# A three-term float32 output projection over 1024 frames: one stage at the end, seven half-size products per column pair instead of eight

## The chip, the cores and the metric

One core of a Trainium2 chip runs the whole layer in one launch. The metric is the device time of that launch in microseconds (us); lower is better.

## The reference, cut to what matters

The layer is a hybrid block: 1024 frames of 2048 features, 16 learned meta frames put ahead of them, one input projection, a causal pooling mixer and a sliding-window attention side by side, gates, and one output projection that is added to the input.

```python
h = concatenate([meta, x])                       # (16 + 1024, 2048)
hn = rmsnorm(h, norm_g)
pv, pg, q, k, v, ag = split(hn @ w_in)           # 1024, 1024, 1024, 128, 128, 1024 columns
pool_out = per group of 256 channels: (trailing mean over 2, 4, 8 or 16 frames - frame) @ pool_w, * pool_scale
attn_out = attention over chunks of 64 frames (own chunk, the one before, the meta frames), q and k
           normalised per head, softmax with a sink logit; 16 query heads, 2 key heads
mixed = concatenate([silu(pg) * pool_out, silu(ag) * attn_out])    # (1024, 2048)
return (h + mixed @ w_out)[16:]                  # w_out is (2048, 2048)
```

All data is float32. The products must keep nearly float32 accuracy, so both kernels split every operand into a high and a low part of the matmul type fp32r and sum three products: high by high, high by low, low by high.

## The kernel before, in words

**Tiling.** The frames are taken in two halves of 512 (the first with the 16 meta frames, 528 columns). Weights come in blocks of 128 rows x 512 columns (256 KB) through four slots: SyncE loads a block into `raw` (`load_block`, L337), ScalarE copies it to `wh` as the high part (`split_high`, L482 through `copy`), VectorE subtracts to get the low part `wl` (`split_low`, L820 through `sub`), and TensorE uses it for 12 matmuls of 512 columns. The splits run three blocks ahead of TensorE (`LEAD`); a load waits until the block four before it is split.

**Order of a half.** The order is written out by hand, engine by engine, in steps of one weight block:

1. *First tiles* (8 blocks, L1231 to L1236): key and value columns. In the first half the frames are transposed on TensorE as they arrive (`first_group`, L1209, four 128x128 transposes per slice k of 128 features), multiplied by the gain on ScalarE (L526) and split on VectorE (L856); this runs four slices ahead. The RMS factor is not applied to the frames: ScalarE sums the squares of each row (`stats`, L495), VectorE inverts (L874), and the factor is spread over the columns (`r_columns`, `r_transposes`, `r_rows`) and multiplied in after the projection.
2. *Query tiles* (32 blocks, L1176 to L1181), with the norms of keys and queries between them.
3. *Four groups* of 24 blocks: gates, pooling inputs, and between the blocks the attention of the group's heads; at the end of each group 12 matmuls of the pooling mixer (L1401 to L1403). GpSimd makes the trailing sums (L443 to L454).
4. *Output projection* (`project`, L1427 to L1429): four column blocks of 512, each over 16 row blocks of `w_out`, for 4 tiles of 128 frames: 4 x 16 x 4 x 3 = 768 matmuls of 128x512. `mixed` is split by `mix_high` and `mix_low`; the residual is added by `add_residual` (L1128) and GpSimd stores the result (L470).

**The second half's frames.** During the first half's output projection they are loaded (L394), normalised in place with their RMS factor and the gain (`stats`, `norm`, L834), transposed (`x_group`, L1192, 16 times four transposes) and split into the same memory as the first half's (`half2_h`, `half2_l`). So the second half needs no factor after the projection.

```python
half2_h = flat_h[:, 0:KT * HALF].rearrange("p (k c) -> p k c", c=HALF)      # rows of 512 columns
act_h = sb("act_h", [P, KT, COLS], f32r)                                    # rows of 528 columns
```

In the first half a matmul reads 512 of the 528 columns of a row, from column 16 on; tiles with the meta frames are two matmuls of 264.

Of the kernel before, what the change touches and what calls it, by code (L numbers as in the profile page):

```python
# [15 lines left out]
P = 128  # L17
D = 2048
KT = D // P
META = 16  # L20
SEQ = 1024
# [3 lines left out]
SUB = COLS // 2  # L25
# [16 lines left out]
YB_FREE = 4  # L42
# [10 lines left out]
OB = D // BLK  # L53
OUT_BLKS = OB * KT
NBLK = IN_BLKS + OUT_BLKS
ROWT = HALF // P
XG = 4

X_LOAD, RES_LOAD = 6, 10
X_AT = (10, 9)  # L60

K_ORDER = [0, 1, 2, 3, 4, 5, 8, 9, 10, 11, 12, 13, 6, 7, 14, 15]
UNITS = 4


FIRST_SPLITS = {0: (0,), 3: (1, 2), 7: (3, 4), 11: (5, 6), 15: (7,)}
FIRST_LOADS = ((0, 2), (2, 4), (4, 8), (8, 12), (12, 16))
# [8 lines left out]
V_N = V_G + KT  # L76


def hymba_layer(nc, xcat, norm_g, w_in, w_out, pool_w, vecs, consts, out):
# [6 lines left out]
    with ctx:  # L86
# [5 lines left out]


        act_h = sb("act_h", [P, KT, COLS], f32r)
        act_l = sb("act_l", [P, KT, COLS], f32r)
# [4 lines left out]
        kT = sb("kT", [P, CHUNK + HALF])  # L100
        vT = sb("vT", [P, CHUNK + HALF])
        k_meta = sb("k_meta", [P, META])
        v_meta = sb("v_meta", [P, META])
        pv_last = sb("pv_last", [P, PAIRS, META])
# [5 lines left out]
        xrs = sb("xrs", [P, 5])  # L110

        band_h = sb("band_h", [P, KVH, (NCH + 1) * BAND], f32r)
        band_x = sb("band_x", [P, KVH, (NCH + 1) * BAND], f32r)
        v_s = sb("v_s", [P, NCH, 2, HD], f32r)
        mix_x = sb("mix_x", [P, 2, BLK], f32r)


        vm = sb("vm", [96, 2, HD], f32r)
        pm = sb("pm", [96, QUAD * P], f32r)
        qs = sb("qs", [P, QUAD, 2, CHUNK], f32r)
        o_part = sb("o_part", [HD, BLK])
        pt = sb("pt", [P, QUAD, 2, P], f32r)
        d_h = sb("d_h", [P, 2, HALF], f32r)
        d_l = sb("d_l", [P, 2, HALF], f32r)
        pw_h = sb("pw_h", [P, BLK], f32r)
        pw_l = sb("pw_l", [P, BLK], f32r)

        pnm = sb("pnm", [P, QUAD, P // QUAD])
        smax = sb("smax", [P, QUAD])
        nmax = sb("nmax", [P, QUAD])
        den = sb("den", [P, QUAD])
        esink = sb("esink", [P, QUAD])
        dtot = sb("dtot", [P, QUAD])
        rden = sb("rden", [P, QUAD])
        hscale = sb("hscale", [P, PAIRS])
        row_buf = sb("row_buf", [P, 2 * COLS])


        scr = sb("scr", [P, 7168])

        x_t = [scr[:, 0:D], scr[:, D:2 * D]]

        x_first = [mixed[:, 4 * r:4 * r + 4, :].rearrange("p k c -> p (k c)") for r in range(ROWT)]
        x_meta = x_t[1][0:META, :]
        meta_sq = x_t[0][0:META, :]
        meta_g = scr[:, 0:KT * META].rearrange("p (k c) -> p k c", c=META)
        g_row = scr[:, 2 * D:3 * D]  # L150
# [4 lines left out]
        res2 = sb("res2", [P, 2, BLK])  # L155
        y = [scr[:, 3 * D:3 * D + BLK], scr[:, 3 * D + BLK:3 * D + 2 * BLK], res2[:, 0, :], res2[:, 1, :]]

        flat_h = act_h[:, :, :].rearrange("p k c -> p (k c)")
        flat_l = act_l[:, :, :].rearrange("p k c -> p (k c)")
        half2_h = flat_h[:, 0:KT * HALF].rearrange("p (k c) -> p k c", c=HALF)  # L160
        half2_l = flat_l[:, KT * COLS - KT * HALF:].rearrange("p (k c) -> p k c", c=HALF)

        def act_cols(h, k, c):

            if h == 0:
                return act_h[:, k, c], act_l[:, k, c]
            own = slice(c.start - META, c.stop - META)
            return half2_h[:, k, own], half2_l[:, k, own]

        mix_h = [band_h[:, 0, 64:64 + BLK], band_h[:, 1, 48:48 + BLK],  # L170
                 v_s[:, 0:4, :, :].rearrange("p c a d -> p (c a d)"),
                 v_s[:, 4:8, :, :].rearrange("p c a d -> p (c a d)")]
        mix_l = [band_x[:, 0, 160:160 + BLK], band_x[:, 1, 144:144 + BLK], mix_x[:, 0, :], mix_x[:, 1, :]]
# [26 lines left out]


# [5 lines left out]
        KB, VB = ((R[0], R[1]), (R[1],)), ((R[2], O), (R[2],))  # L207
# [4 lines left out]
        YB = [R[0][:, :], S[:, 0, :], S[:, 1, :], O]  # L212
        FB = [S[:, 0, :], S[:, 1, :], PT[:, :], PM[:, :]]
        XB = [R[1][:, :], R[2][:, :], PT[:, :], PM]

        ident = cst[:, C_ID:C_ID + P]

# [4 lines left out]
        s_g = sem("s_g")  # L222
# [3 lines left out]
        s_x = [sem(f"s_x{i}") for i in range(2)]  # L226
        s_raw = [sem(f"s_raw{i}") for i in range(RAW)]
        s_pw = sem("s_pw")
        s_res = [sem(f"s_res{i}") for i in range(ROWT)]
        s_out = [sem(f"s_out{i}") for i in range(ROWT)]  # L230
        s_last = sem("s_last")
        s_free = sem("s_free")
# [12 lines left out]
        s_xn = sem("s_xn")  # L245
# [59 lines left out]
        s_me = sem("s_me")  # L305
        s_mh = sem("s_mh")
        s_ml = sem("s_ml")
        s_y = sem("s_y")
        s_ye = sem("s_ye")
# [3 lines left out]
                    s_ex, s_pl, s_pve, s_pvr, *s_gv, *s_gt, s_free]  # L313

        block = ctx.enter_context(nc.Block())

        def product_done(eng, h, n):

            eng.wait_ge(s_blk, ONE + h * NBLK + n + TILE_BLKS)

# [11 lines left out]
        def _(sp):  # L332
# [14 lines left out]

            sp.dma_start(cst[:, 0:P], consts[:, 0:P]).then_inc(s_id, 16)
# [13 lines left out]
            for h in range(HALVES):  # L362
                h0 = h * NBLK
                for n in range(RAW if h == 0 else 0, KV_BLKS):
                    load_block(h0 + n, n % RAW, w_in[TILE_BLKS * (n % 2) + n // 2, :, :])
                with sp.Fori(0, PAIRS) as j:
# [4 lines left out]
                sp.wait_ge(s_free, ONE + h * OB * ROWT)  # L371
                with sp.Fori(0, GROUPS) as g:

# [6 lines left out]

                def out_loads(nb, frames):

                    for k in range(KT):
                        kk = K_ORDER[k]
                        load_block(h0 + IN_BLKS + nb * KT + k, k % RAW,
                                   w_out[kk * P:(kk + 1) * P, bass.ds(nb * BLK, BLK)])
                        if k == X_LOAD and frames is not None:

                            sp.wait_ge(s_me, ONE + (h + 1) * 2 * GROUPS)
                            sp.wait_ge(s_xt, 1 + XG * (ROWT - 1 + nb))  # L390
                        if X_LOAD <= k < X_LOAD + OB and frames is not None:

                            cols = slice((k - X_LOAD) * BLK, (k - X_LOAD + 1) * BLK)
                            sp.dma_start(x_t[frames][:, cols],  # L394
                                         xcat[bass.ds(HALF + META + P * nb, P), cols]).then_inc(s_x[frames], 16)
                        if k == RES_LOAD:

                            sp.wait_ge(s_me, ONE + (h + 1) * 2 * GROUPS)

                            sp.wait_ge(s_free, ONE + (h * OB + nb) * ROWT)  # L400
# [5 lines left out]
                if h == 0:  # L406
                    with sp.Fori(0, 2) as i:
                        for v in range(2):
                            nb = i * 2 + v
                            out_loads(nb, v)  # L410
# [1098 lines left out]
```

## Time and profile before

| | before |
|---|---|
| median of 3 runs | 1246.59 us (1245.5 to 1247.13) |
| profiled execution, its own time | 1246.73 us |
| its span, first to last instruction | 1244.9 us |
| TensorE busy | 1232.2 us, 99% |
| VectorE / ScalarE busy | 63% / 51% |
| DMA, mean | 108 GB/s |
| first half: first tiles, queries, groups, output projection end at | 42, 139, 461, 643 us |
| second half: first tiles, queries, groups, output projection end at | 665, 757, 1067, 1241 us |

In the windows of rows 3, the first is a stretch of the second half's groups, the second the last output stage, the third what is left after TensorE's last matmul. In the timeline a matmul's duration contains its pipeline; its price in a stream is the distance from its start to the next start. "Idle before" is an engine's gap ahead of an instruction, with what ended it.

### The profile page before, as it was taken

What the parts mean: (1) busy time and instruction counts of PE and PEld (TensorE: products, weight loads), DVE (VectorE), ACT (ScalarE), POOL (GpSimd) and SP (SyncE); (2) the same over time, 40 slices, a digit from 0 to 9 for tenths busy, and PEclk for the clock granted to TensorE, in tenths of its full rate; (3) what the DMA queues carried; (4) which work ended last, traced back from release to release, by engine and by line L of the source; (5) the groups of instructions that cost most, each with busy time, mean ns of one, the idle gap of its engine ahead of it and who ended that gap; (6) DMA issues with size and microseconds to landing.
All of it is one profiled execution on the core that took longest, in us unless ns stands there. A gap on an engine that the chain in (4) does not pass through costs nothing.

```text
span 1244.9 us, 19321 instructions
## 1 busy us (share of the span) xinstructions
PE 1232.2 (99%) x6210; PEld 1043.4 (84%) x6210; DVE 788.4 (63%) x1381; ACT 638.2 (51%) x1495; POOL 81.5 (7%) x94
## 2 busy tenths in 40 slices
PE   8999999999999999999999999999999999999998
PEld 7887798898988978888888888888888888888887
DVE  4677767576675775665644676675757657654553
ACT  4744465464564655545533444655646556444442
POOL 0000001020120210000000000000101103000000
PEclk9999999999999999999999999999999999999999
DMA  7223323322232225544533333332322322343442
GB/s 239 77 85 102 92 78 86 83 85 78 76 94 78 74 71 207 192 133 150 193 127 85 99 95 94 78 92 76 102 77 85 91 79 88 117 133 127 168 144 85
DMA packets 72817, 134.38 MB, mean 108 GB/s; under 512 B 8096, under 2 KB 11424, under 8 KB 72608
## 3 DMA queue, kind: packets, MB, share of 16 engines
q1 hardware_dynamic: 70368, 125.17, 33.0%
q0 software_dynamic: 2384, 8.39, 1.9%
q8 instruction: 35, 0.57, 0.2%
q14 instruction: 30, 0.25, 0.1%
HBM read 125.14 MB, written 8.39 MB: 107 GB/s over the span
## 4 chain that ended last, share of the span: by engine, by line
PE 93%; DVE 3%; ACT 2%; DMA 1%; issue 1%; SPq 0%; DVEq 0%; ACTq 0%
PE R L1176 16%; PE R L1177 16%; PE R L1181 16%; PE S L1427 5%; PE S L1429 5%; PE S L1428 5%; PE R L1429 2%; PE R L1427 2%; PE OP L1427 2%; PE OP L1429 2%; PE R L1428 2%; PE OP L1428 2%; PE OP L1352 1%; PE S L1327 1%; PE OP L1177 1%; PE OP L1176 1%
## 5 line engine op out<-in xcount | busy, mean ns | idle before, releaser
L482 ACT ACTIVATE wh<-raw 128x512 fp32r<-128x512 f32 x400 | 249.9, 630 | 428.6 <-PE R L1181 197.9
L820 DVE TENSOR_TENSOR wl<-raw,wh 128x512 fp32r<-128x512 f32 x400 | 279.7, 701 | 289.3 <-ACT wh L482 288.9
L1176 PE MATMUL R<-act_h,wh 128*128 128x512 f32 (+1 forms) x1056 | 385.3, 370 | 1.2 <-DVE wl L820 1.1
L1177 PE MATMUL R<-act_l,wh 128*128 128x512 f32 (+1 forms) x1056 | 381.5, 366 | 0.0
L1181 PE MATMUL R<-act_h,wl 128*128 128x512 f32 (+1 forms) x1056 | 365.1, 365 | 0.0
L1176 PEld LDWEIGHTS R<-act_h,wh 128*128 128x128 f32 x1056 | 198.7, 188 | 33.2 <-DVE wl L820 2.0
L1177 PEld LDWEIGHTS R<-act_l,wh 128*128 128x128 f32 x1056 | 198.7, 188 | 30.3
L1181 PEld LDWEIGHTS R<-act_h,wl 128*128 128x128 f32 x1056 | 190.2, 188 | 33.1
L454 POOL TENSOR_TENSOR scr<-scr 128x527 f32<-128x527 f32 (+3 forms) x40 | 50.2, 1254 | 379.2 <-ACT scr L482 325.5
L482 ACT ACTIVATE pm<-OP 16x128 fp32r<-16x128 f32 x256 | 68.3, 267 | 5.5
L820 DVE TENSOR_TENSOR pt<-PT,pt 128x512 fp32r<-128x512 f32 x32 | 22.1, 692 | 59.9 <-ACT pm L482 59.9
L943 DVE RECIPROCAL scr<-scr 128x512 f32<-128x512 f32 x16 | 53.5, 3346 | 3.2 <-ACT scr L634 2.4
L820 DVE TENSOR_TENSOR qs<-mixed,qs 64x256 fp32r<-64x256 f32 x64 | 26.9, 421 | 39.6 <-ACT qs L482 39.1
L1427 PE MATMUL S<-wh,band_h 128*128 128x512 f32 x128 | 49.9, 390 | 0.0
L1427 PE MATMUL S<-wh,v_s 128*128 128x512 f32 x128 | 49.9, 390 | 0.0
L1429 PE MATMUL S<-wh,band_x 128*128 128x512 f32 x128 | 49.9, 390 | 0.0
L1429 PE MATMUL S<-wh,mix_x 128*128 128x512 f32 x128 | 49.9, 390 | 0.0
L1428 PE MATMUL S<-wl,v_s 128*128 128x512 f32 x128 | 49.8, 389 | 0.0
L1428 PE MATMUL S<-wl,band_h 128*128 128x512 f32 x128 | 49.8, 389 | 0.0
L701 ACT ACTIVATE scr<-S,nmax 128x144 f32<-128x144 f32 x128 | 47.0, 379 | 0.7
L820 DVE TENSOR_TENSOR mix_x<-mixed,v_s 128x512 fp32r<-128x512 f32 x64 | 43.8, 684 | 0.0
L820 DVE TENSOR_TENSOR band_x<-mixed,band_h 128x512 fp32r<-128x512 f32 x64 | 43.8, 684 | 0.0
(249 smaller groups left out, 1996.0 us busy)
## 6 DMA issues: line engine op xcount, KB each, us to landing
raw<-w_in_blocks SPq DMA_DIRECT2D x272, 256.0 KB, 2.6
raw<-w_out_in SPq DMA_DIRECT2D x128, 256.0 KB, 3.0
scr<-xcat SPq DMA_DIRECT2D x32, 256.0 KB, 4.4
res<-xcat SPq DMA_DIRECT2D x16, 256.0 KB, 3.2
out<-scr POOLq DMA_DIRECT2D x14, 256.0 KB, 2.7
out<-res POOLq DMA_DIRECT2D x14, 256.0 KB, 4.5
mixed<-xcat SPq DMA_DIRECT2D x3, 1024.0 KB, 10.8
scr<-pool_w_in SPq DMA_DIRECT2D x8, 256.0 KB, 3.3
```

Of the source, the lines that this page charges most:

```text
L454: ins = pool.tensor_tensor(dst[:, lo:COLS], src[:, lo:COLS], src[:, lo - step:COLS - step], ALU.add)
L482: return nc.scalar.activation(dst, src, ACT.Copy)
L701: nc.scalar.activation(prob[:, c, :], S[:, c // 2, (c % 2) * KEYS:(c % 2 + 1) * KEYS], ACT.Exp, bias=nmax[:, c:c + 1], accum_out=den[:, c: ...
L820: return nc.vector.tensor_tensor(dst, a, b, ALU.subtract)
L943: nc.vector.reciprocal(q_rs[t % 2], q_rs[t % 2]).then_inc(s_qrs, 1)
L1176: mm(o, wh[:, b, w], xh, start=(k == 0), stop=False)
L1177: mm(o, wh[:, b, w], xl, start=False, stop=False)
L1181: last = mm(o, wl[:, b, w], xh, start=False, stop=(k == KT - 1))
L1327: last = mm(o, q, band_x[:, e, at], start=False, stop=not masked)
L1427: mm(YB[r], mh, wh[:, k % SPLIT, :], start=(k == 0), stop=False)
L1428: mm(YB[r], mh, wl[:, k % SPLIT, :], start=False, stop=False)
L1429: last = mm(YB[r], ml, wh[:, k % SPLIT, :], start=False, stop=(k == KT - 1))
```

## The change

The output projection of the first half is taken out; one stage at the end computes all 1024 frames. With A11, A12 (first half, pooling and attention features; `a1`), A21, A22 (second half; `mixed`) and the quarters B11 to B22 of `w_out` for a pair of column blocks, seven products take the place of eight, in the order Q4 = A22 T4, P1 = A11 B11, Q5 = S5 T5, P2 = A12 B21, Q6 = S6 T6, Q7 = S7 T7, Q3 = S3 B22. There are two passes (column pairs) of 7 x 8 blocks, 112 blocks of 12 matmuls.

- The sums of frames S5, S6, S7, S3 are made on VectorE in SBUF (32 subtractions of 128x512). Results are combined by 48 additions per pass on VectorE; P1 is copied out by ScalarE.
- The sums of weights T5, T6, T4, T7 are made in outer memory (`wsum`) by DMAs that GpSimd issues at the end of each of the eight groups: 4 DMAs of 1 MB each time, a plain copy and an accumulating one by turns.
- `mixed` of the first half is written to outer memory group by group (`spill`) and the second half's frames are loaded into the tiles that come free (`next_frames`); `mixed` comes back as `a1` during the first output blocks.
- The second half's frames are handled like the first's: transposed inside the first tiles (`first_group(1, k)`, now three slices ahead, with three PSUM banks), gain on ScalarE, split on VectorE, squares summed after the last slice, factor applied after the projection.
- Rows of `act_h` and `act_l` are 576 columns apart and read from column 64 on; a pad precedes them. The meta tiles are two matmuls of 272 and 256.

```diff
-SUB = COLS // 2
+SUB = 272
+ROW, META_AT = 576, 48
...
+FIRST_SPLITS = ({0: (0,), 3: (1, 2), 7: (3, 4), 11: (5, 6), 15: (7,)},
+                {3: (3,), 7: (4,), 11: (5, 6), 15: (7,)})
...
+            def spill(q):
+                sp.wait_ge(s_me, ONE + 2 * (q + 1))
+                sp.wait_ge(s_oe, ONE + UNITS * (q + 1))
+                for t in (2 * q, HK + 2 * q):
+                    sp.dma_start(mx0[t:t + 2, :, :].rearrange("k p c -> p k c"), mixed[:, t:t + 2, :]).then_inc(s_sp, 16)
...
                 for n in range(RAW if h == 0 else 0, KV_BLKS):
                     load_block(h0 + n, n % RAW, w_in[TILE_BLKS * (n % 2) + n // 2, :, :])
+                if h:
+                    spill(GROUPS - 1)
+                    for b in range(TILE_BLKS):
+                        load_block(h0 + KV_BLKS + b, b % RAW, w_in[KV_BLKS + b, :, :])
+                        if b == 1:
+                            next_frames(GROUPS - 1)
...
+                        if h == 0 and g and b == 6:
+                            spill(g - 1)
+                        if h == 0 and g and b == 14:
+                            next_frames(g - 1)
...
+                        if add:
+                            pool.dma_start(wsum[kind, p, rows, :], src, accum_op=ALU.add).then_inc(s_t[kind], 16)
...
+            WSUMS = ((T5, "B11", False), (T5, "B12", True), (T6, T5, False), (T6, "B22", True),
+                     (T4, T6, False), (T4, "B21", True), (T7, "B12", False), (T7, "B22", True))
...
+            for i in range(ROWT):
+                for p in range(PASSES):
+                    at = p * PASS + i
+                    todo[at + 12].append((q4_out, p, i))
+                    todo[at + 16].append((c11_p1, p, i))
+                    todo[at + 20].append((q4_p1, p, i))
+                    todo[at + 24].append((q5_out, p, i))
+                    todo[at + 32].append((c11_out, p, i))
+                    todo[at + 40].append((q6_out, p, i))
+                    todo[at + 44].append((v_add, p, i))
+                    todo[at + 48].append((q7_out, p, i))
...
+            for k in range(HK):
+                todo[4 + k].append((sum5, k))
+                todo[12 + k].append((sum6, k))
+                todo[20 + k].append((sum7, k))
+                todo[28 + k].append((sum3, k))
...
+            def first_group(h, k):
...
+                    if k % 4 == 0:
+                        pe.wait_ge(s_xc, 32 * (k // 4 + 1))
+                    if k == 0:
+                        pe.wait_ge(s_ex, ONE + GROUPS * UNITS * (QUAD + 1))
+                    elif k == 2:
+                        pe.wait_ge(s_oe, OE[0])
+                    elif k > 2:
+                        pe.wait_ge(s_xl, x_turn(h, k - 3) + 1)
...
+                        if n % 2 == 0 and k + ahead < KT:
+                            first_group(h, k + ahead)
```

## Rows read from the trace of the kernel before

**Rows 1.** The page, busy time and share of the span by engine.

```profile
PE 1232.2 (99%) x6210; PEld 1043.4 (84%) x6210; DVE 788.4 (63%) x1381; ACT 638.2 (51%) x1495; POOL 81.5 (7%) x94
```

**Rows 2.** The page, chain that ended last, by engine.

```profile
PE 93%; DVE 3%; ACT 2%; DMA 1%; issue 1%; SPq 0%; DVEq 0%; ACTq 0%
```

**Rows 3.** Windows: span, busy (count) of PE, PEld, DVE, ACT, POOL; clock; DMA; GB/s.

```profile
842.00:919.00 77.00, 77.00 (x377) 64.69 (x376) 49.41 (x108) 43.42 (x123) 5.03 (x4) 1.00 0.29 86
...
1067.20:1241.50 174.30, 174.27 (x769) 144.00 (x767) 89.55 (x139) 69.21 (x120) 6.52 (x12) 1.00 0.39 129
...
1243.90:1244.90 1.00, 0.00 (x0) 0.00 (x0) 0.00 (x0) 0.00 (x0) 0.00 (x0) 0.50 0.00 0
```

**Rows 4.** Timeline, TensorE, first half's queries, first and last of 48 (start, duration).

```profile
59.07 0.40 PE L1176 MATMUL R<-act_h,wh 128*128 128x512 f32 x1
...
69.98 0.39 PE L1181 MATMUL R<-act_h,wl 128*128 128x512 f32 x1
```

**Rows 5.** Timeline, TensorE, pooling mixer of the first half, first and last of 8.

```profile
459.29 0.39 PE L1402 MATMUL PT<-d_l,pw_h 128*128 128x512 f32 x1
...
460.87 0.39 PE L1403 MATMUL R<-d_h,pw_l 128*128 128x512 f32 x1
```

**Rows 6.** Timeline, TensorE, 264-column matmuls; the second row ends a run of 48.

```profile
36.01 0.28 PE L1231 MATMUL R<-act_h,wh 128*128 128x264 f32 x1
...
41.87 0.39 PE L1176 MATMUL S<-act_h,wh 128*128 128x512 f32 x1
```

**Rows 7.** Timeline, TensorE, one `x_group` in the first half's output projection.

```profile
634.20 0.39 PE L1429 MATMUL OP<-wh,band_x 128*128 128x512 f32 x1
...
634.78 0.48 PE L1427 MATMUL R<-wh,band_h 128*128 128x512 f32 x1
635.10 0.40 PE L1428 MATMUL R<-wl,band_h 128*128 128x512 f32 x1
```

**Rows 8.** Timeline, VectorE, in the last output stage.

```profile
1106.17 0.69 DVE L820 TENSOR_TENSOR wl<-raw,wh 128x512 fp32r<-128x512 f32 x1 [1.43 <-ACT wh L482]
1106.78 0.68 DVE L820 TENSOR_TENSOR band_x<-mixed,band_h 128x512 fp32r<-128x512 f32 x1
1108.90 0.69 DVE L1128 TENSOR_TENSOR scr<-R,scr 128x512 f32<-128x512 f32 x1 [1.44 <-PE R L1429]
```

**Rows 9.** Timeline, VectorE, the end of the first half's last group.

```profile
459.49 0.42 DVE L1053 SCALAR_TENSOR_TENSOR mixed<-scr 128x256 f32<-128x256 f32 x1
```

**Rows 10.** Timeline, first half's start: last transposes, their split, then ScalarE to the factor's rows.

```profile
32.63 0.60 PE L1209 MATMUL OP<-cst,mixed 128*128 128x128 f32 x4
...
33.99 0.75 DVE L856 SCALAR_TENSOR_TENSOR act_l<-OP,vec,act_h 128x512 fp32r<-128x512 f32 x1 [0.42 <-ACT act_h L526]
...
39.02 0.61 ACT L482 ACTIVATE wh<-raw 128x512 fp32r<-128x512 f32 x1
...
48.01 0.61 ACT L482 ACTIVATE wh<-raw 128x512 fp32r<-128x512 f32 x1
...
52.35 0.63 ACT L482 ACTIVATE wh<-raw 128x512 fp32r<-128x512 f32 x1
```

**Rows 11.** SyncE's queue, two DMA issues, then the page's landing time of 512 KB frame loads.

```profile
466.45 0.33 SPq L394 DMA_DIRECT2D scr<-xcat  x1
467.03 0.36 SPq L337 DMA_DIRECT2D raw<-w_out_in  x1
...
mixed<-xcat SPq DMA_DIRECT2D x2, 512.0 KB, 5.0
```

**Rows 12.** Weight loads by tile, from 0 to 14 us, when the DMA engines were full.

```profile
DMA to landing us min/median/max: 3.9/8.2/11.1
```

**Rows 13.** Timeline, TensorE, four transposes early in the span.

```profile
12.83 1.11 PE L1209 MATMUL S<-cst,mixed 128*128 128x128 f32 x4
```

**Rows 14.** Timeline, GpSimd, and the page's landing time of its 1 MB DMA.

```profile
418.27 0.22 POOL L443 TENSOR_TENSOR pv_last<-scr,row_buf 128x16 f32<-128x16 f32 x1 [58.25 <-ACT scr L482]
...
scr<-norm_g_in POOLq DMA_DIRECT2D x1, 1024.0 KB, 6.4
```

More of the change, by code:

```diff
@@ L110, in hymba_layer @@
         xrs = sb("xrs", [P, 5])
[L115 to L126, printed above, removed]
@@ L144, in hymba_layer, with sbi @@
[L144 to L148, printed above, removed]
-        meta_g = scr[:, 0:KT * META].rearrange("p (k c) -> p k c", c=META)
-        g_row = scr[:, 2 * D:3 * D]
+        hscale = sb("hscale", [P, PAIRS])
+        pad = sb("pad", [P, PAD // 4])
+        inner = ExitStack()
+        def sbi(name, shape, dt=f32):
+            return inner.enter_context(nc.sbuf_tensor(name, shape, dt))
@@ L159, in hymba_layer @@
[L159 to L172, printed above, removed]
@@ L173, in hymba_layer, with act_cols @@
-        mix_l = [band_x[:, 0, 160:160 + BLK], band_x[:, 1, 144:144 + BLK], mix_x[:, 0, :], mix_x[:, 1, :]]
+        def act_cols(k, c):
+            at = slice(META_AT + c.start, META_AT + c.stop)
+            return act_h[:, k, at], act_l[:, k, at]
         k_sq, k_rs = scr[:, 0:528], scr[:, 528:1056]
@@ L225, in hymba_layer @@
         s_xg = sem("s_xg")
-        s_x = [sem(f"s_x{i}") for i in range(2)]
+        s_xc = sem("s_xc")
+        s_sp = sem("s_sp")
         s_raw = [sem(f"s_raw{i}") for i in range(RAW)]
         s_pw = sem("s_pw")
[L229 to L232, printed above, removed]
         s_init = sem("s_init")
@@ L379, in _ @@
                         load_block(h0 + n, b % RAW, w_in[n, :, :])
[L381 to L400, printed above, removed]
-                        if RES_LOAD <= k < RES_LOAD + ROWT:
-                            r = k - RES_LOAD
-                            sp.dma_start(y[r], xcat[h * HALF + META + P * r:h * HALF + META + P * (r + 1),
-                                                    bass.ds(nb * BLK, BLK)]).then_inc(s_res[r], 16)
@@ L545, in _ @@
                 copy(ones_r, cst[:, C_BLK:C_BLK + P]).then_inc(s_ones, 1)
-                for s in range(5 if h == 0 else 0, KV_BLKS):
+                for s in range(5, KV_BLKS):
                     split_high(h4, s + LEAD)
-                    if h == 0 and s < 7:
-                        first_stats(s - 3)
+                    if s < 7:
+                        first_stats(h, s - 3)
                 if h == 0:
@@ new lines, in q3_out @@
+            def q3_out(p, r):
+                if p == PASSES - 1 and r < ROWT - 1:
+                    dve.wait_ge(s_y, r + 1)
+                else:
+                    product_out(p, Q3)
+                dve.wait_ge(s_v12, p * ROWT + r + 1)
+                add(c1[:, r, :], bank(p, Q3, r), c1[:, r, :]).then_inc(s_c12, 1)
+            todo = {n: [] for n in range(OUT_BLKS)}
+            for i in range(ROWT):
+                for p in range(PASSES):
+                    at = p * PASS + i
[7 more added lines that the diff above has]
+                    todo[at + 48].append((q7_out, p, i))
+                    todo[at + 56 if p < PASSES - 1 else OUT_BLKS - 1].append((q3_out, p, i))
@@ L1187, in _ @@
             own = (slice(META, COLS),)
-            def x_group(slot, q):
-                for kk in range(4):
-                    k = 4 * q + kk
-                    last = nc.tensor.transpose(XB[q][:, kk * P:(kk + 1) * P],
-                                               x_t[slot][:, k * P:(k + 1) * P], ident)
-                last.then_inc(s_xt, 1)
             pe.wait_ge(s_id, 16)
@@ L1368, in group @@
                         when[0] = [(sum_squares, PAIRS - 1)]
+                    if h == 0 and isinstance(g, int) and g == GROUPS - 1:
+                        for k in range(2):
+                            when.setdefault(21 + k, []).append((next_frames, k))
                     def events(s):
```

828 lines of the change are left out of this document (497 added, 331 removed).

## The prediction

> **What bounds the kernel now.** I read the busy shares first: TensorE is busy 1232.2 of 1244.9 us, the next engine 63% [rows 1]. Then the chain that ended last: 93% of it is TensorE [rows 2]. Then the windows: in a stretch of the groups and in the last output stage TensorE is busy without a hole, at full clock, with DMA at 29% and 39% [rows 3]. So the time is the number of matmuls times their start-to-start distance, plus the few holes at stage boundaries. An engine beside it counts only where it makes TensorE late. Two distances matter. In the last output stage 174.30 us over 769 matmuls is 0.2267 each [rows 3]. In the first half's queries 47 distances fill 10.91 us, 0.2321 each [rows 4]: the same shape, 2.4% dearer.
>
> **Matmuls removed.** Before: 2 stages x 768 = 1536. After: 7 products x 2 passes x 8 blocks x 12 = 1344. 192 fewer at 0.2267 is **-43.5 us**. Nothing hides this; every one stood on the full engine.
>
> **Rows of 576 columns.** The first half has 384 + 4 x 192 = 1152 matmuls of 512 columns that read `act_h` and `act_l`. After, each row starts on a multiple of 256 bytes, as the second half's did before. That the operand is what makes them dearer, and not the half, is borne out by the pooling mixer of the same half, which reads `d_h`: 7 distances in 1.58 us, 0.2257 each [rows 5]. I take the whole: 1152 x 0.0054 = **-6.2**; bounds -6.2 and 0 (the new rows could stand as badly for another reason).
>
> The meta tiles: 96 + 384 = 480 pairs, now 264 + 264 at 0.1221 each, 48 in 5.86 us [rows 6], after it 272 + 256. The columns are the same in number. If they too get the good price (528 columns at 0.2267/512), 480 x 0.0104 is -5.0; if the 272 costs its 8 columns more and the 256 saves nothing, +1.7. I take **0**: the rows show 264-column ones only misaligned, and a short matmul may be held by something else.
>
> **The second half's transposes.** Sixteen sets of four leave the first half's output stage, where a set puts 0.58 - 0.23 and 0.32 - 0.23 between its neighbours, 0.44 in all [rows 7]; sixteen enter the second half's first tiles: **0** net as work. What they wait for there is new.
>
> **The second half's start.** Before, its operands were ready during the output stage. After, nothing stands between the first half's last mixer matmul (461.1) and the first tiles, and every wait there is TensorE's.
> - Slice 2 goes into bank O, after the last attention output, 459.9 [rows 9] (459.49 + 0.42). VectorE still has some six operations of 0.6 to 0.75 before slice 2's split: **+0.8**, bounds 0 and 2.
> - Slices 12 to 15 wait for the last quarter of the frames. SyncE issues it only after weight block 9, whose slot is free when block 5 is split, which on ScalarE and VectorE comes behind slice 11. In the first half the split of a slice ends 2.1 us after its transposes start and the next is 0.6 later [rows 10] (32.63 to 33.99 + 0.75), so 2.7. Three issues at about 0.55 [rows 11] (466.45 to 467.03) bring 1.1 more, 3.8; such a load lands in 5.0 [rows 11]: 8.8 after slice 11's transposes. TensorE has 0.35 + 3 x 0.23 = 1.1 of work. **+7.7**; bounds 5 and 13 (landings below). Behind that wait in TensorE's queue stands the rest of the half.
> - The clock. After TensorE's last matmul the granted clock is 0.50 in the last microsecond [rows 3], and four transposes take 1.11 early on against 0.60 warm [rows 10, 13]. An idle time of 7.7 us is long enough for that as far as these rows go: **+2.5**, bounds 0 and 4.
> - Slice 15 late: **+0.3**. The first query block needs `wh`, which ScalarE copies 6.4 us after slice 15's transposes [rows 10] (32.63 to 39.02), plus two copies of `kT` and `vT` and VectorE's split: 8.3, against 5.4 of work on TensorE (it ran four slices ahead before, three now, and its blocks are short): **+2.9**.
> - The factor's rows: in the first half ScalarE is at them from 39.02 to 48.01 [rows 10], 9.0 us, less 0.4 for two meta copies; that puts the transposes of the factor at 15.4 against TensorE's 13.8: **+1.7**, and 0.9 for these eight transposes themselves. The squares of the keys, 48.01 to 52.35 [rows 10]: **+0.6**.
> - The splits of `mixed` leave the end of the first half's last group: **-0.5** of a hole of 1.0. The second half's groups now multiply by the factor on VectorE and ScalarE as the first half's do: **+1.0**.
>
> Together +17.9.
>
> **The output stage.** A block is 12 x 0.2267 = 2.72 us. VectorE needs two splits, 0.61 start to start [rows 8] (1106.17 to 1106.78), and in about 40 of the 112 blocks two more operations of 0.61 to 0.69: 2.6 at most, under 2.72, with a lead of three blocks. ScalarE has about 1.7. Loads run four blocks ahead, 10.9 us, against landings whose median is 8.2 with the DMA engines full [rows 12]. I price it at **0**: what covers it is that lead; if it is gone, see rival C.
>
> **GpSimd's copies.** 4 MB at the end of each group, hidden behind a group's 77 us of matmuls: before, DMA is at 29% and 86 GB/s there [rows 3], and a 1 MB transfer on this queue lands in 6.4 us [rows 14]. GpSimd waits for the copy made two steps earlier before it issues its accumulating one, and its own next sums come after a hole of 58.25 us [rows 14]. **0**; see E.
>
> Sum: -43.5 - 6.2 + 17.9 = **-31.8**. The profiled execution took 1246.73, 0.1 over the median; 1246.73 - 31.8 = 1214.9, told as **1215**.
>
> **Rivals.**
> **A, no late frames** (the load of block 9 is issued sooner than I count, say by ScalarE running ahead): -7.7 and -2.5, about **1205**. Against it: the split of block 5 is behind slice 11 in both engines' written order. 0.08.
> **B, slow landings.** The frames and weight blocks of the start share the DMA engines with GpSimd's 4 MB accumulation, issued just before. With the engines full, weight blocks landed in a median of 8.2 and at most 11.1 us [rows 12], against the 5.0 I use: +3 to +6 on the last quarter, and as much on blocks that follow, **1218 to 1226**. For it: the group's copy is issued at the end of the group. Against: most of it may be through. 0.15. The Trainium skill, page "DMA: Bandwidth & Descriptors", section "Issuing engines are not separate DMA queues", says that DMAs of all issuing engines run on the same 16 engines and interleave; by that the 4 MB are in the way of SyncE's loads though they are on GpSimd's queue, which speaks for B; by it the time is B's.
> **C, VectorE becomes the bound of the output stage.** If its operations stand 0.69 apart (their full duration [rows 8]) and not 0.61, a block of four with its waits is 2.8 to 2.86 against 2.72, over 40 blocks **+5**, about **1220**. For it: its operations wait for TensorE's banks at just that time. Against: the lead. 0.12.
> **D, the alignment gives nothing**: +6.2, **1221**. 0.08.
> **E, slower than before: GpSimd's queue blocks.** The trailing sums stand behind a wait for the group before's copy. If 4 MB through outer memory take longer than a group and the slack, 77 us [rows 3] and most of the 58 us hole [rows 14], some 132 us (under 32 GB/s), TensorE waits at the mixer of each group. It has to cost over 31.8 us in seven groups, 4.6 each, so 137 us a copy, 31 GB/s; at 142 us a copy **1253**. Against it: the 1 MB in 6.4 us [rows 14] is 160 GB/s. 0.05. That the change doesn't do what it says would need a product more; the loops give 2 x 56 blocks of 12 matmuls, so I give that no chance of its own.
>
> **How the numbers follow.** The forecast 0.52, A 0.08, B 0.15, C 0.12, D 0.08, E 0.05. The forecast's own range: -5.0 or +1.7 (meta tiles), -2.7 to +5.3 (last quarter), -2.5 to +1.5 (clock), and the rest +-2, which don't all fall on one side: 1207 to 1222. The range over all goes to A and to the upper end of B and of B with C: 1205 to 1229. About 0.2%, 2.5 us, is what a measurement of this kernel can tell from no change; only E, or B, C and D together with the bounds at their worst, come within it or above: faster 0.92, same 0.03, slower 0.05.
>
> **What the profile of after would show.** Right: some 6020 matmul records (6210 less 192); first-half queries at 0.227 apart; one hole of 7 to 8 us on TensorE before slice 12's transposes, put down to a DMA on SyncE's queue, with a lower granted clock behind it; holes of 3 and 2 us after it; an output stage of 1344 x 0.2267 = 305 us without holes. Wrong: a second hole of that size, matmuls of the output stage waiting for VectorE or for `raw`, or mixer matmuls that wait for GpSimd. The prediction fails altogether if the output stage takes over 340 us.

## The result, and the profile after

The changed kernel takes **1223.42 us** (median of 4 runs, 1223.19 to 1225.02) against 1246.05 (4 runs, 1245.12 to 1247.13): ratio 0.982, 95% interval 0.980 to 0.984. That is 22.6 us faster, where 31.6 were forecast; it lies within the stated range and 8.4 us above the forecast. The profiled execution's span is 1221.2 us, 23.7 less than before.

The page of the changed kernel, busy time by engine and the chain by engine, beside [rows 1, 2]:

```profile
PE 1191.3 (98%) x6026; PEld 1009.2 (83%) x6026; DVE 835.9 (68%) x1464; ACT 629.5 (52%) x1480; POOL 118.0 (10%) x133
...
PE 77%; DVE 9%; ACT 7%; DMA 4%; issue 3%; SPq 0%; DVEq 0%; ACTq 0%
```

There are 6026 matmul records, 6210 - 192 and 8 for the transposes of the factor in the second half; some 6020 were foreseen. But the chain is 77% TensorE now and was 93%: it leaves TensorE where TensorE waits. Where that is, a table by stage says; the windows are cut at TensorE's own landmarks. Before: the first half to its mixer's end, its output stage, the second half up to its first group, its groups, the last output stage (columns: bounds, length, busy us and count of PE, PEld, DVE, ACT, POOL, clock, DMA share, GB/s):

```profile
0.00:461.10 461.10, 452.54 (x2599) 395.51 (x2600) 312.48 (x565) 251.72 (x633) 40.74 (x45) 1.00 0.32 94
461.10:643.08 181.98, 181.98 (x833) 150.45 (x832) 110.28 (x167) 90.62 (x158) 7.72 (x14) 1.00 0.49 160
643.08:766.07 122.99, 122.54 (x545) 100.87 (x543) 75.14 (x82) 50.84 (x91) 1.68 (x4) 1.00 0.33 99
766.07:1067.23 301.16, 300.93 (x1469) 252.54 (x1470) 200.31 (x431) 175.76 (x495) 24.80 (x20) 1.00 0.30 87
1067.23:1241.50 174.27, 174.24 (x769) 144.00 (x767) 89.52 (x139) 69.21 (x120) 6.52 (x12) 1.00 0.39 129
```

After, the same stages, with no output stage in the middle:

```profile
0.00:457.85 457.85, 448.32 (x2608) 395.12 (x2608) 311.68 (x564) 251.17 (x633) 53.90 (x61) 1.00 0.49 141
457.85:607.28 149.43, 135.11 (x608) 109.69 (x606) 91.37 (x107) 72.10 (x131) 0.00 (x0) 0.95 0.36 99
607.28:912.84 305.56, 303.10 (x1468) 252.16 (x1469) 212.69 (x445) 175.89 (x492) 48.94 (x44) 1.00 0.49 134
912.84:1217.65 304.81, 304.81 (x1345) 252.23 (x1343) 219.40 (x349) 130.32 (x227) 15.20 (x28) 1.00 0.52 163
```

First half -3.3; output work 181.98 + 174.27 to 304.81, of which 7.1 us of transposes went to the next stage (16 sets at 0.45 [rows 7]), so -44.3; the second half's start 122.99 to 149.43, +26.4, or +19.3 without those transposes; its groups +4.4. The last output stage is full: 1345 matmuls in 304.81 us, 0.2266 each. The start of the second half is not: TensorE is busy 135.11 of 149.43, at a mean clock of 0.95. Four of TensorE's waits in the changed kernel (us in total, times, longest; what is left out here is the 4.5 us at the very start, 4.4 before, and some of 1.7 us in total or less):

```profile
PE S L1382 <- DMA mixed<-xcat: 8.8, 1, 8.8
...
PE S L1346 <- DVE wl L915: 3.5, 1, 3.5
PE OP L1526 <- DVE pm L915: 2.1, 4, 1.5
...
PE PT L1582 <- DVE d_l L915: 1.6, 2, 1.0
```

The timeline of TensorE at the first two of these:

```profile
484.17 1.11 PE L1382 MATMUL S<-cst,mixed 128*128 128x128 f32 x4 [8.76 <-DMA mixed<-xcat]
...
501.60 0.76 PE L1346 MATMUL S<-act_h,wh 128*128 128x512 f32 x1 [3.55 <-DVE wl L915]
502.16 0.63 PE L1347 MATMUL S<-act_l,wh 128*128 128x512 f32 x1
502.58 0.63 PE L1351 MATMUL S<-act_h,wl 128*128 128x512 f32 x1
...
505.33 0.39 PE L1346 MATMUL S<-act_h,wh 128*128 128x512 f32 x1
```

The second of these, before the first query block, is called the query hole below. Its 3.5 us is idle time; from start to start, less one matmul, it is 3.7 (497.67 to 501.60), and the first hole is 8.9. Slice 12's transposes take 1.11 behind the long hole, as those of [rows 13]. Behind the query hole the granted clock is 0.50 from 501.60 to 504.70 and matmuls of 512 columns stand 0.43 apart instead of 0.227, half speed, until 505.10: nine distances in 3.73 us where 2.04 would do, 1.7 us lost.

### The profile page after: what moved, and what is told of

Read it like the earlier page. It is cut to its first block, busy times and chain, and to the rows that moved or that the text cites. A ratio compares the mean times of both kernels' runs of the same rounds, so it can differ in the third digit from the quotient of the medians.

```text
span 1221.2 us, 17852 instructions
## 1 busy us (share of the span) xinstructions
PE 1191.3 (98%) x6026; PEld 1009.2 (83%) x6026; DVE 835.9 (68%) x1464; ACT 629.5 (52%) x1480; POOL 118.0 (10%) x133
## 4 chain that ended last, share of the span: by engine, by line
PE 77%; DVE 9%; ACT 7%; DMA 4%; issue 3%; SPq 0%; DVEq 0%; ACTq 0%
PE R L1346 13%; PE R L1351 13%; PE R L1347 13%; PE R L1631 3%; PE R L1630 3%; PE R L1632 3%; DMA raw<-w_in_blocks 2%; ACT pm L596 2%; PE OP L1631 2%; PE OP L1630 2%; PE S L1631 2%; PE S L1630 2%; PE OP L1632 2%; PE S L1632 2%; DVE wl L915 2%
## 5 line engine op out<-in xcount | busy, mean ns | idle before, releaser
L1346 PE MATMUL R<-act_h,wh 128*128 128x512 f32 (+2 forms) x1056 | 384.9, 369 | 1.7 <-DVE wl L915 1.7
L1347 PE MATMUL R<-act_l,wh 128*128 128x512 f32 (+2 forms) x1056 | 378.4, 364 | 0.0
L1351 PE MATMUL R<-act_h,wl 128*128 128x512 f32 (+2 forms) x1056 | 364.9, 365 | 0.0
L1346 PEld LDWEIGHTS R<-act_h,wh 128*128 128x128 f32 x1056 | 198.5, 188 | 31.6 <-DVE wl L915 2.5
L1632 PE MATMUL R<-wh,mix_l 128*128 128x512 f32 x168 | 65.4, 390 | 0.0
L1630 PE MATMUL R<-wh,mix_h 128*128 128x512 f32 x168 | 65.4, 389 | 0.0
L1631 PE MATMUL R<-wl,mix_h 128*128 128x512 f32 x168 | 65.4, 389 | 0.0
L559 POOL TENSOR_TENSOR scr<-scr,row_buf 128x528 f32<-128x528 f32 (+1 forms) x16 | 22.3, 1395 | 405.0 <-ACT scr L596 359.0
L1631 PE MATMUL OP<-wl,mix_h 128*128 128x512 f32 x112 | 43.6, 390 | 0.0
L1630 PE MATMUL S<-wh,mix_h 128*128 128x512 f32 x112 | 43.6, 390 | 0.0
L1632 PE MATMUL OP<-wh,mix_l 128*128 128x512 f32 x112 | 43.6, 389 | 0.0
## 6 DMA issues: line engine op xcount, KB each, us to landing
wsum<-w_out_in POOLq DMA_DIRECT2D x24, 1024.0 KB, 17.5
```

The costliest lines, as they stand in the source:

```text
L559: pool.tensor_tensor(pv[jj][:, scaled], pv[jj][:, scaled], rb[:, scaled], ALU.mult).then_inc(s_pvr, 1)
L1346: mm(o, wh[:, b, w], xh, start=(k == 0), stop=False)
L1347: mm(o, wh[:, b, w], xl, start=False, stop=False)
L1351: last = mm(o, wl[:, b, w], xh, start=False, stop=(k == KT - 1))
L1630: mm(banks[r], mh, wh[:, slot, :], start=(k == 0), stop=False)
L1631: mm(banks[r], mh, wl[:, slot, :], start=False, stop=False)
```

## The experiments

All are the changed kernel with one edit, unless said otherwise. The gains are differences to the 1223.42 us above. The kernel before ran beside each of three batches of them, at 1244.79, 1245.73 and 1246.06 us, and the changed kernel did not; so a gain of a few microseconds is uncertain by about 1.

**The frames' load ahead of two weight blocks** (`frames_early`).

```diff
                     spill(GROUPS - 1)
+                    next_frames(GROUPS - 1)
                     for b in range(TILE_BLKS):
                         load_block(h0 + KV_BLKS + b, b % RAW, w_in[KV_BLKS + b, :, :])
-                        if b == 1:
-                            next_frames(GROUPS - 1)
```

> SyncE issues the last quarter of the second half's frames right behind the last spill, before the loads of weight blocks 8 and 9; nothing else moves. Theory (the load's place in SyncE's order is the cause of the 8.8 us hole): the spill's issue at 462.7 and its landing of 5.6 put the frames' issue near 468.5, landing 5 to 6.5 later, 474 to 475, against TensorE's arrival at 475.2. The hole shrinks to 0 to 1 us and the 1.8 us at the lower clock behind it go, so 9 to 10.7 us less: 1213 to 1214.5 us. The hole of 3.7 before the first query block stays. Rival (the transfer itself is slow, whatever its place, because the spill and GpSimd's copies fill the DMA engines): it lands in 10 us or more and a hole of over 3 us stays: 1217 or more.

Measured: 1216.17 us (1214.31 to 1216.98), 7.3 less. SyncE's issue of the frames, in the changed kernel and then here, and TensorE's arrival here:

```profile
477.28 0.89 SPq L409 DMA_DIRECT2D mixed<-xcat  x2
```

```profile
471.26 0.89 SPq L409 DMA_DIRECT2D mixed<-xcat  x2
...
476.80 0.66 PE L1381 MATMUL S<-cst,mixed 128*128 128x128 f32 x4 [1.76 <-DMA mixed<-xcat]
```

The order of SyncE's queue was the cause. 1.8 us of the hole stay, because the spill took up to 8.5 us to land where 5.6 was counted, so that the issue came at 471.3 and not 468.5. The query hole stayed at 3.6 us, as foreseen, with a longer stretch at half speed behind it than in the changed kernel (13 matmuls against 8). These two are why the time lies above the 1213 to 1214.5 of the theory.

**Block 8 split before the sums of squares** (`block8_first`).

```diff
-                {3: (3,), 7: (4,), 11: (5, 6), 15: (7,)})
+                {3: (3,), 7: (4,), 11: (5, 6), 15: (7, 8)})
```

> In the second half ScalarE and VectorE split weight block 8 right after block 7, ahead of the sums of squares; nothing else moves. Theory 1 (the weight split behind two sums of squares is the cost): the hole of 3.7 us before the first query block and 1.6 us at the lower clock go, 1218 us. Theory 2 (ScalarE's chain of four sums of squares, roots and copies ends at 508.7 whatever stands first in it, and TensorE's transposes of the factor need its end): the hole moves to the transposes of the factor, 4 to 5 us of it, and the time stays within 1 to 2 us of the changed kernel: 1221.5 to 1224.

Measured: 1223.28 us (1223.16 to 1224.01), nothing. Neither theory had the place right; the second had the sense. ScalarE splits blocks 7 and 8 and then begins the squares:

```profile
492.52 1.14 ACT L596 ACTIVATE wh<-raw 128x512 fp32r<-128x512 f32 x2
493.56 1.90 ACT L610 ACTIVATE row_buf<-mixed 128x2048 bf16<-128x2048 f32 x1
```

TensorE runs block 8 without a wait and stops before block 9 instead:

```profile
503.39 0.50 PE L1347 MATMUL S<-act_h,wh 128*128 128x512 f32 x1 [3.50 <-DVE wl L916]
```

So what stands first in ScalarE's work behind slice 15 does not count. That its length does is what the next edit tries.

**Sums of squares in parts** (`stats_parts`, `stats_parts2`). ScalarE's chain itself is shortened: three quarters of each row are there long before, so their squares are summed in its idle time inside the first tiles. The edit also splits blocks 8 and 9 earlier (for block 8, this alone gave nothing above).

```diff
+                    if h and k == 6:
+                        ...
+                        nc.scalar.activation(junk[:, 0:1], eps, ACT.Sqrt).then_inc(s_table, 1)
+                    for r in {6: (0,), 10: (1,), 14: (2, 3)}.get(k, ()) if h else ():
+                        stats_a(r)
...
-                first_stats(h, 0)
-                first_stats(h, 1)
+                    stats_b(0)
+                    stats_b(1)
+                    split_high(h4, 9)
+                    stats_b(2)
+                    stats_b(3)
```

> In the second half the squares of three quarters of each row are summed inside the first tiles (after slices 6, 10 and 14), the table of the root is loaded there too, and only the last quarter stands behind slice 15; weight blocks 8 and 9 are split ahead of or between these. The sums are the same but for their order. Theory (ScalarE's chain from slice 15 to the factor's columns is what TensorE waits for, some 14 us of it): the chain ends about 5 us earlier, the hole of 3.5 us at the first query blocks and the 1.6 us at the lower clock behind it go, and no wait over 1 us takes their place: 1218 us. Rival (the hole only moves on, to the transposes of the factor, as it moved one block on with block 8 split first): 1221 to 1223.5.

Measured: **1234.80 us** (1234.23 to 1236.65), 11 us slower, though the 3.5 us hole is gone from its profile. The loss is spread over the whole kernel. A window of 100 us of the output stage, of which the edit touches nothing, in this kernel:

```profile
930.00:1030.00 100.00, 100.00 (x430) 80.49 (x429) 77.94 (x125) 42.86 (x76) 2.26 (x4) 1.00 0.55 171
```

and in the changed kernel:

```profile
930.00:1030.00 100.00, 100.00 (x443) 82.86 (x442) 81.03 (x130) 44.19 (x78) 2.25 (x4) 1.00 0.55 176
```

The counts take in matmuls that lie across the ends of the window; from start to start it is 0.2333 per matmul against 0.2267 (means over the output stage). Each of the two small tiles that the edit adds takes 32 bytes and the pad had been made only 32 smaller, so every later tile had moved by 32 bytes. With the pad cut by 32 bytes more, which is all that changes:

> The kernel with the sums of squares in parts, with one number changed: the pad ahead of the frames' rows is 260 bytes and not 292. There the two new small tiles and the pad had put the frames' rows, and the operands of the output stage, 32 bytes further on than in the changed kernel (a multiple of 32 bytes and no longer of 128); now they stand where they did. Theory (the shift by 32 bytes made every matmul that reads them about 6 ns dearer and hid the gain): matmuls of the output stage go from 0.2333 back to 0.2267, 9 us, those of the halves likewise, 14 us in part; the holes at the first query blocks stay away: 1218 us. Rival (summing in parts costs the 11 us itself, elsewhere): over 1230.

Measured: **1218.59 us** (1217.35 to 1218.79), 4.8 less than the changed kernel and 16.2 less than with the shift; the same window holds 442 matmuls again. So 32 bytes of address cost 16. The output stage, from its first matmul to its last, shows it best: 304.42 us in the changed kernel and in every other kernel whose tiles stand where its tiles do, 313.36 in the two with the shift (`stats_parts` and, below, `best1`).

The 4.8 us understate what the shorter chain is worth. Between the same matmuls, the second half's start is 7.4 us shorter than in the changed kernel, 5.4 of it at the query hole and the half speed behind it. But the first half, which the edit leaves alone, is 3.3 longer in this profile. 2.2 of that are at a pooling mixer, where the changed kernel's hole is 1.0 us; here it is 1.9, and matmuls at half speed follow:

```profile
376.21 0.50 PE L1621 MATMUL PT<-d_h,pw_h 128*128 128x512 f32 x1 [1.88 <-DVE d_l L951]
...
377.31 0.63 PE L1621 MATMUL PT<-d_h,pw_h 128*128 128x512 f32 x1
377.74 0.63 PE L1622 MATMUL PT<-d_l,pw_h 128*128 128x512 f32 x1
```

What makes this hole comes under `pitch`.

**The operands' start alone** (`misaligned`). `META_AT` is 32 instead of 48: reads start 64 bytes off.

> The frames' rows keep their distance of 576 columns but are read from column 48 on instead of 64, so their starts are multiples of 64 bytes and not of 256; all that is computed stays. Theory (the start of the moving operand's row is what made the first half's matmuls dearer before): 96 + 2 x 1152 = 2400 matmuls of 512 columns go from 0.227 to 0.232 to 0.233 each, +12 to +14.5 us: 1235.5 to 1238. Rival (the first half was dearer for another reason, as the rows' distance): the time stays at 1223.4 and the distances at 0.227.

Measured: 1237.71 us (1234.78 to 1239.84), +14.3. Six distances in the first half's queries, in the changed kernel and then here:

```profile
63.33 0.39 PE L1351 MATMUL R<-act_h,wl 128*128 128x512 f32 x1
...
64.69 0.39 PE L1351 MATMUL R<-act_h,wl 128*128 128x512 f32 x1
```

```profile
63.69 0.39 PE L1346 MATMUL R<-act_h,wh 128*128 128x512 f32 x1
...
65.09 0.39 PE L1346 MATMUL R<-act_h,wh 128*128 128x512 f32 x1
```

0.2267 against 0.2333. A matmul's recorded duration is 0.39 in both: only the distance shows it. So the start address counts. But it isn't the whole rule. In the kernel before, rows are 2112 bytes apart, and as the program is built slices 1, 5, 9 and 13 start on multiples of 256 bytes. The three matmuls of slice 1 in one of its first half's query tiles:

```profile
59.77 0.40 PE L1176 MATMUL R<-act_h,wh 128*128 128x512 f32 x1
...
60.48 0.40 PE L1176 MATMUL R<-act_h,wh 128*128 128x512 f32 x1
```

That is 0.71 for three. Over all its first half's tiles such a slice takes 0.70, the slices that start 128 bytes past a multiple of 256 take 0.69, and in the changed kernel a slice takes 0.68 (the first slice of a tile left out). Why rows that start well are dear there too, no run here tells.

**Rows of the sums of weights 576 columns apart** (`pitch`), and **no sums at all** (`no_sums`, which leaves out the sums of weights and loads rows of `w_out` in their place, not of the input weights as the text below has it).

```diff
-        wsum = nc.dram_tensor("wsum", (4, PASSES, D // 2, BLK), f32).ap()
+        wsum = nc.dram_tensor("wsum", (4, PASSES, D // 2, BLK + 64), f32).ap()[:, :, :, 0:BLK]
```

> The rows of the sums of weights in outer memory are 576 columns apart instead of 512, so that no copy between them is one contiguous stretch; the same bytes move. Theory (the copies from sum to sum go out in packets of 32 KB, 128 packets for 4.19 MB, and weight loads stand behind them: landing 14.4 us at most, ScalarE waits 4.0 us, TensorE 1.2 and 0.7 at the pooling mixer in just the two groups with such a copy): both holes go, 1221.5 us, and the landings of weights in that stretch stay under 8 us. Rival (it is the amount and not the packets): the holes stay and the time is the same, 1223.4.

> GpSimd issues none of the sums of weights, and the output stage loads rows of the input weights in their place (the sums of weights are left out, the same bytes are loaded). Theory (the sums cost only by single late loads): the 1.2 and 0.7 us at the pooling mixer go and about 1 us of the frames' landing: 1220.5 to 1222 us, 1 us or less beside the kernel with the pitch of 576. Rival (32 MB of copies and accumulations slow matmuls or loads all along): 1217 or less.

Measured: 1220.13 us (1219.19 to 1221.01) with the pitch and 1220.05 (1219.36 to 1221.77) without the sums: no difference that the runs can tell, with about 1 us of doubt, since the two ran in different batches. So of the sums' cost of about 3 us, most comes back when the same bytes are moved in smaller packets. In the changed kernel, from 355 to 377 us, GpSimd's queue sent its 4.19 MB in 128 packets, and ScalarE waited for a weight block:

```profile
q0 software_dynamic: 128, 4.19, 55.4%
```

```profile
372.55 0.63 ACT L596 ACTIVATE wh<-raw 128x512 fp32r<-128x512 f32 x1 [4.04 <-DMA raw<-w_in_blocks]
```

That is the hole of 1.0 us before the mixer (374.56). The landings of weight blocks from 340 to 385 us (min, median, max), in the changed kernel and then with the pitch, where the copy is 1088 packets:

```profile
DMA to landing us min/median/max: 2.5/3.2/14.4
```

```profile
DMA to landing us min/median/max: 2.6/3.9/9.7
```

The theory wanted these landings under 8 us, and the worst was 9.7. But with the pitch no hole is left before either mixer: from start to start that is 1.2 and 0.7 us. The rest of its 3.3 us is not put down to single waits here.

The amount of data has an effect all the same, at the end of the first half, where GpSimd's copies fill the DMA engines together with the last spill. The spill's landing in the changed kernel and then without the sums (with the pitch it is 7.4 to 8.8):

```profile
DMA to landing us min/median/max: 7.0/7.6/8.3
```

```profile
DMA to landing us min/median/max: 3.9/4.3/4.8
```

In these kernels the frames wait longer for their turn in SyncE's queue than for the spill, and it costs little: their hole is 8.8 us in the changed kernel and 8.1 without the sums. Where they are issued right behind the spill, as in `frames_early`, its landing is what they wait for.

**The last group** (`mix_early`, `tanh_late`). Its hole of 1.5 us (1.6 from start to start) before the value matmuls at 906.55 has two candidates: the splits of `mixed`, and ScalarE's wait for VectorE before the third gate's tanh.

```diff
-                            for n, s in enumerate((21, 22, 24)):
+                            for n, s in enumerate((18, 19, 24)):
```

> In the last group of the second half the first two splits of mixed move from steps 21 and 22 to steps 18 and 19 on ScalarE and VectorE; nothing else moves. Theory (those splits stand ahead of the last attention tile's p_high and p_low, and make the hole of 1.6 us before its value matmuls at 906.5): the hole shrinks to the 0.3 to 0.5 that the other groups have, 1.1 to 1.3 us less: 1222.2 us. Rival (ScalarE's wait for VectorE's multiplication by the factor, 3.0 us before its tanh at 900.1, makes it): the hole stays over 1.2 us and the time at 1223.4.

```diff
-                    todo[20].append((gate_tanh, 2, R[0]))
                     todo[21].append((d_high, 1))
+                    todo[22].append((gate_tanh, 2, R[0]))
...
-                    todo[21].append((gate_out, 2))
+                    todo[23].append((gate_out, 2))
```

> In every group the third gate's tanh moves on ScalarE from step 20 to step 22, behind the last attention tile's p_high, and its use on VectorE from step 21 to 23; nothing else moves. Theory (ScalarE stands before that tanh until VectorE has multiplied the gate by the factor, and the split of the weights and p_high stand behind it): the holes before the value matmuls go, 1.6 us in the last group and 0.3 in the others: 1221 us. Rival (p_high waits for the transposes on TensorE or for VectorE anyway): within 0.5 us of 1223.4.

Measured: 1223.20 us (1222.3 to 1225.31) for the first, nothing, and 1220.44 (1217.77 to 1221.11) for the second, 3.0 less. In its profile the holes before the value matmuls of the eight groups are 3.7 us shorter together, but the late weight block of `pitch` costs 2.1 us more than in the changed kernel at the first half's mixer and 0.9 more at the second half's. The tanh on ScalarE in the changed kernel, with the weight split that stands behind it:

```profile
900.08 0.63 ACT L833 ACTIVATE row_buf<-scr 128x512 f32<-128x512 f32 x1 [3.01 <-DVE scr L1146]
900.61 0.62 ACT L596 ACTIVATE wh<-raw 128x512 fp32r<-128x512 f32 x1
```

The same with the splits moved forward; VectorE is later for them and ScalarE waits longer:

```profile
900.94 0.63 ACT L833 ACTIVATE row_buf<-scr 128x512 f32<-128x512 f32 x1 [4.27 <-DVE scr L1146]
```

With the tanh behind `p_high`, the value matmuls follow the matmul before them with 0.41 between the starts:

```profile
903.88 0.39 PE L1351 MATMUL R<-act_h,wl 128*128 128x512 f32 x1
904.29 0.75 PE L1526 MATMUL OP<-pt,v_s 128*128 128x256 f32 x4
```

**Together** (`best1`, `best2`).

> The early load of the last quarter of the frames, the pitch of 576 in outer memory, the sums of squares in parts with blocks 8 and 9 split earlier, and the earlier splits of mixed, together. If the four costs lie one behind the other on TensorE they add: 1223.4 - 7.3 - 3.3 - 5.3 - 1.2 = 1206.3 us. If the end of one wait only brings the next (ScalarE's chain with less time to hide in, since TensorE arrives 9 us earlier): 1209 to 1212.

Measured: 1225.32 us (1224.56 to 1226.9). It carries the 32-byte shift of `stats_parts` and the splits that gained nothing.

> The early load of the last quarter of the frames, the pitch of 576 in outer memory, the sums of squares in parts with the pad of 260, and the later tanh, together. If the costs lie one behind the other they add: 1223.4 - 7.3 - 3.3 - 5.3 - 2.0 = 1205.5 us, 1204 to 1208. If not, 1209 or more, with the waits that took their place in the profile.

Measured: **1202.42 us** (1202.13 to 1204.15), ratio to the kernel before 0.965 (0.964 to 0.967): 43.6 us faster than before and 21 faster than the change as it was made. Page, TensorE's longest waits behind the 4.5 us at its start, and clock:

```profile
PE 1184.5 (99%) x6026; PEld 1006.5 (84%) x6026; DVE 836.3 (70%) x1465; ACT 631.3 (53%) x1489; POOL 119.1 (10%) x133
```

```profile
PE S L1420 <- DMA mixed<-xcat: 2.1, 1, 2.1
PE R L1384 <- DVE wl L950: 1.7, 2, 0.8
PE OP L1502 <- DVE d_l L950: 1.2, 2, 0.6
```

```profile
core 0: 1200.4 us, clock 1.000
```

The single gains add to 7.3 + 3.3 + 4.8 + 3.0 = 18.4; together they are 21.0. Two things that the traces show work that way. The stretch at half speed behind the query hole, which grew when the frames came early, is gone. And `stats_parts2` and `tanh_late` each lost over 2 us at the mixer to the late weight block, which the pitch takes away. The wait of 2.1 us for the frames is left: the last spill lands up to 9.0 us after its issue and the frames are issued behind it. That it would go if the spill landed in under 5 us, as it does without the sums, is an expectation and not tested.

## Why the prediction was right or wrong, point by point

By stage the gain of 31.8 fell short by 7.9: 3.4 in the first half, 1.9 in the second half's start and 3.4 in its groups, less 0.8 in the output work. The mechanisms of the large terms were right.

- **Matmuls removed**: right. -44.3 by the windows against -43.5; most of the 0.8 between them is that the first half's output stage had been a little dearer than the last (181.98 - 7.1 = 174.9 against 174.27).
- **Rows of 576 columns**: right in the price (0.2321 to 0.2267 in the queries) and in the sense, since `misaligned` shows that the start of the operand's rows counts. The reason given is wrong in part: the prediction said that the rows now start on multiples of 256 bytes, as the second half's did. As the program is built both start 128 bytes past one, and have the good price; moved by 64 or 32 they lose it; and a quarter of the slices of the kernel before did start on multiples of 256 and did not have it. The first half as a whole gained 3.3 of the 6.7 forecast (6.2 and the 0.5 of its last group). Of what is missing, 1.2 us is the step **"GpSimd's copies: 0"**, at the mixer at 374.56, and 0.9 is three holes of 0.3 before value matmuls that the prediction had no term for; the rest is open. The meta tiles at 0: right; a pair costs 0.246 after and cost 0.247 before (means of the distances in the first half's groups, 384 pairs).
- **The frames' load**: right, and undersized: 8.8 us for 7.7. The order in SyncE's queue was as counted, and the issue came 3.2 us after slice 11's transposes began (3.8 was counted); the second of the two loads took 6.4 us to land and not 5.0.
- **The clock behind it**: 1.8 for 2.5.
- **The first query block**: the step that failed first. "ScalarE copies it 6.4 us after slice 15's transposes" was read in the first half; here it was 8.0 (492.16 to 500.12). 0.3 of the difference are the copies of `kT` and `vT`, which the prediction counted apart. 1.3 it did not have: in the first half ScalarE had loaded the root's table in the first microseconds, and here a load of 1.28 us stands in the chain:

```profile
495.70 0.19 ACT L610 ACTIVATION_READ_ACCUMULATOR row_buf<-mixed 128x1 f32 x1
495.91 1.28 ACT L616 ACT_TABLE_LOAD   x1
```

  The hole was 3.7 for 2.9 (from start to start), and the 1.7 us at half speed behind it had no term at all: the prediction charged the clock once, for the long hole, and not for the next one. In return the transposes of the factor waited 0.1 and not 1.7, since TensorE came to them that much later. Start of the second half: 19.3 for 17.4.
- **"The second half's groups: +1.0"**: the worst step, +4.4. It was taken from a likeness with the first half, and not from a chain. Most of the price is an order: the gate now passes VectorE before its tanh, and on ScalarE the weight split and `p_high` stand behind that tanh. The holes before the value matmuls of these four groups are 2.5 us together, from start to start, where the kernel before had one of 0.35; `tanh_late` takes 2.3 of them away. 0.7 more is the second late weight block (675.09). The remaining 1.5 or so is open.
- **The output stage at 0**: right, 304.81 us without a hole, and so rival C did not come.
- **GpSimd's copies at 0**: wrong by about 3 us, and mostly in a way that none of the rivals had: two copies with large packets, each behind a group's pooling. Rival B counted on the amount of data at the second half's start. By the Trainium skill (page "DMA: Bandwidth & Descriptors", section "Issuing engines are not separate DMA queues") the copies do share the engines with SyncE's loads. The trace agrees: weight loads landed up to 14.4 us after their issue, and the last spill in 7.0 to 8.3 where it takes 3.9 to 4.8 without the copies. So B's mechanism was there, but on the spill, where SyncE's order hid it; the frames themselves landed 1.4 us later than counted, and B's time of 1218 to 1226, in which the result lies, does not come from it.
- **Rivals A, D, E**: the frames were late, the alignment counted, and GpSimd never held up the sums by a whole copy. E's time is also added up wrongly: from 132 us a copy on, 142 is 10 us in each of seven groups, 1285 us and not 1253.

## What to carry to other kernels

A stage that only prepares the next one hides more than its own work: when it is taken out, list every queue whose operations had run under it, and follow each to the engine that now waits, including what stands behind a wait in written order. Here, moving the first item of a late chain moved the hole by one block, and doing the chain's early part while its engine was idle removed it. A single edit's time can hide its gain, when a wait elsewhere grows in the same run: compare the stages, between the same matmuls. And after any edit that adds a tile, read the distance between matmuls in a stage that the edit does not touch: 32 bytes cost more here than any wait.

## What the runs showed of the hardware that was not expected

- The start address of what a matmul reads changes its price. Matmuls of 512 columns stand 0.2267 us apart in the changed kernel, whose operands start 128 bytes past a multiple of 256, and 0.2333 where they are moved by 32 (`stats_parts`) or 64 bytes (`misaligned`); the engine shows as 100% busy in both. A multiple of 128 alone does not give the good price: the kernel before had such slices at 0.230 to 0.234 a matmul.
- Copies from outer memory to outer memory whose rows lie end to end went out in packets of 32 KB (128 for 4.19 MB), and 256 KB loads of another queue landed up to 14.4 us after their issue; in 1088 packets the worst was 9.7, and no matmul waited.
- Accumulating and plain copies of 1 MB, four issued at a time, landed in a median of 17.5 us. Two stores of 512 KB beside them landed in 7.0 to 8.3 us, without them in 3.9 to 4.8 (`no_sums`).
- Behind a hole of 3.5 us TensorE ran 8 matmuls at half speed. Behind one of 1.76 us (`frames_early`, 476.80) it ran none, and behind one of 1.88 (`stats_parts2`, 376.21) seven: a hole's length alone did not say which.
